# One block instead of three and a loop for a whole model, its weights fetched across the stages

## The reference, cut to what matters

```
for l in 0, 1:
    h = rmsnorm(x, norm_mix[l])
    u, q_lat, kv_lat, k_rope, hq, hf, hi, hg, gate_logits = split(h @ w_in[l])
    x += (g0 * s5(u) + g1 * mla(q_lat, kv_lat, k_rope) + g2 * hgrn2(hq, hf, hi, hg)) @ w_out[l]
    x += cross_attention(rmsnorm(x, norm_cross[l]), rmsnorm(mem, norm_mem[l]))   # keys: mem_n @ x_w_kv
    x += swiglu(rmsnorm(x, norm_ffn[l]), w_gate_up[l], w_down[l])
x = rmsnorm(x, norm_final)
for l in 0, 1:                                  # l = 0 the even part, l = 1 the odd part
    shift, scale, gate = split(silu(c) @ w_ada[l] + b_ada[l])     # "adaption"
    h = rms_norm(x, g[l]) * (1 + scale) + shift
    x += gate * (attention_l(h) @ w_out_l)      # even: sliding window and block-sparse; odd: block-sparse
out = rms_norm(x, final)
```

## Time and profile before

| what | before |
|---|---|
| median of 3 runs | 1708.95 us (1707.45 to 1709.88) |
| the profiled execution's own time | 1706.99 us |
| its span, first to last instruction | 1705.2 us |
| PE busy | 1633.9 us, 96% of the span |
| DVE, ACT, POOL busy | 837.5, 425.9, 9.1 us |
| mean granted clock of PE | 0.983 |
| moved by DMA | 244.16 MB, mean 143 GB/s |

### The profile page before, as it was taken

The page is one execution under the profiler, slowest core; times in us unless marked ns, Lnnn a source line. Parts: engine busy times, 40 slices in busy tenths (PEclk is TensorE's granted clock), DMA queues, the critical chain, the costliest instruction groups (busy, mean ns, idle before and its releaser), DMA issues. The chain is left out here.

```text
span 1705.2 us, 25659 instructions
## 1 busy us (share of the span) xinstructions
PE 1633.9 (96%) x10243; PEld 1378.0 (81%) x10243; DVE 837.5 (49%) x1646; ACT 425.9 (25%) x883; POOL 9.1 (1%) x24
## 2 busy tenths in 40 slices
PE   6999999999899998999999999899999899899997
PEld 5878868888899997868867888899998767676776
DVE  5346782324656754345792223667663454322332
ACT  5523423103111002423423203100001144411331
POOL 1000000000000001000000000000000000000000
PEclk9999999999999999999999999999999999899998
DMA  8442252353368553533352443467553525123310
GB/s 263 159 148 99 90 184 100 100 185 111 127 202 264 198 175 107 205 114 105 130 152 86 148 148 98 150 198 248 193 178 124 196 74 198 50 99 125 117 56 25
DMA packets 177659, 244.16 MB, mean 143 GB/s; under 512 B 22245, under 2 KB 100734, under 8 KB 177534
## 3 DMA queue, kind: packets, MB, share of 16 engines
q1 hardware_dynamic: 177534, 242.44, 42.6%
HBM read 241.37 MB, written 1.05 MB: 142 GB/s over the span
## 5 line engine op out<-in xcount | busy, mean ns | idle before, releaser
L566 PE MATMUL psum<-hT,ring 128*128 128x256 f32 (+1 forms) x2576 | 575.4, 383 | 9.1 <-DVE hT L2503 7.6
L566 PEld LDWEIGHTS psum<-hT,ring 128*128 128x128 f32 (+1 forms) x2576 | 488.0, 191 | 88.3 <-issue 20.1
L451 DVE TENSOR_TENSOR psum<-psum,const 128x512 f32<-128x512 f32 (+2 forms) x40 | 22.1, 570 | 162.7 <-PE psum L380 154.8
L1261 PE MATMUL psum<-hT,ring 128*128 128x128 f32 x704 | 86.4, 283 | 7.6 <-issue 7.6
L1261 PEld LDWEIGHTS psum<-hT,ring 128*128 128x128 f32 x704 | 84.4, 200 | 8.4 <-issue 8.4
L566 PE MATMUL psum<-uT,ring 128*128 128x256 f32 x384 | 85.6, 381 | 0.0
L566 PEld LDWEIGHTS psum<-uT,ring 128*128 128x128 f32 x384 | 72.5, 190 | 10.9 <-issue 0.7
L1446 ACT ACTIVATE SCR<-SCR 128x512 f32<-128x512 f32 x22 | 13.9, 630 | 223.8 <-DVEq L1886 223.8
L577 PE MATMUL psum<-ring,hT 128*128 128x512 f32 (+3 forms) x224 | 68.1, 459 | 0.0
L429 ACT ACTIVATE SCR<-psum,stats 128x128 f32<-128x128 f32 (+2 forms) x128 | 49.6, 398 | 44.9 <-DVE stats L465 39.0
L1643 DVE COPY_PREDICATED SCR<-levels,psum 128x512 f32<-128x512 uint8 x32 | 23.5, 734 | 73.8 <-PE psum L1025 73.1
(11 more groups left out here) (424 smaller groups left out, 2491.6 us busy)
## 6 DMA issues: line engine op xcount, KB each, us to landing
ring<-in_w_in SPq DMA_DIRECT2D x48, 1024.0 KB, 7.2
ring<-in_ffn_w_gate_up SPq DMA_DIRECT2D x88, 512.0 KB, 6.3
ring<-in_w_ada SPq DMA_DIRECT2D x24, 1024.0 KB, 5.9
ring<-in_ffn_w_down SPq DMA_DIRECT2D x16, 1024.0 KB, 8.0
ring<-in_w_in_odd SPq DMA_DIRECT2D x16, 1024.0 KB, 7.4
ring<-in_w_in_even SPq DMA_DIRECT2D x10, 1024.0 KB, 7.3
ring<-in_x_w_kv SPq DMA_DIRECT2D x8, 1024.0 KB, 5.2
ring<-in_ssm_w_glu SPq DMA_DIRECT2D x8, 1024.0 KB, 6.5
```

The costliest lines, as they stand in the source:

```text
L451: ins = nc.vector.tensor_tensor(pick(view), pick(view), mask[:, heads], ALU.add)
L566: ins = nc.tensor.matmul(b[0:width, n * S:n * S + S], w[k // 4][:, k % 4, c0[n]:c0[n] + width], src[:, k, :], start=k == 0, stop=k == kt - 1)
L1261: ins = nc.tensor.matmul(b[:, at:at + P], left, right, start=first, stop=last)
```

## The change

**One block.** `build` makes all job lists and the ring's list once, numbered on across the stages, and all stages stand in one `nc.Block`, with no barrier, loop or clearing of semaphores. Each stage has its own named semaphores. The parameters of layer 1 (`par[1]`) and of the second block are transposed in step 11 of the feed-forward before (job `next params`).

**Ring.** SP runs through one list of 232 pieces. The last pieces of layer 0 are followed by layer 1's kx, hf, hq, ql, whose slots come free with d12, d13 and d14; those of layer 1 by ada10, ada11, ada12 (two pieces each) and qa, of which ada12.1, qa.0 and qa.1 have slots that d14 frees. In the feed-forward the list is now `gate_up(0)`, six adaption pieces, `gate_up(1)`, and so on; so ff1.0 has the slot of ff0.0 and ff1.1 that of ff0.1.

**Start.** SP: half the constants, x, 15 small transfers, then the ring's hf.0 and hf.1, mem, other constants, raw b and c, then hq, kx, then levels, positions, the second block's parameters, ql and so on. PE: x0 to x3, params, square x, hf0, mem0 to mem3, square mem (from squares that ACT writes), hf1, hq0, hq1, kx0 left, kx0 right, kx1. DVE copies x out of PSUM and makes the rotary angles after its parameter chain; ACT copies and squares mem after its own parameter chain and hf0.

**Layer 1.** Order: kx0 left, square x, kx0 right, kx1, hf. Square x has 4 tiles: ACT squares x as the down steps finish it, DVE adds pairs. The memory's norm for layer 1 stands in down step 12.

**Adaption.** Three jobs a layer in the norm gap before the feed-forward (one before `square xf`'s sums, two behind), with their transposes in steps 0, 1, 2. Of the second block's six, three stand around its first squares, one in attention step 13, two behind `square 2`.

**Second block and end.** `square 0` and `square 1` have 4 tiles each. The output leaves in four DMAs of 256 KB, each behind its copy. As the jobs are numbered on across the stages, other jobs than before are the ones that need two successive banks at the turn of the six (mla1; c6, c7 before; mla3 in layer 0, a1 and b2's compression after).

The diff, cut to its core and with changes of indentation left out:

```diff
     def load(self, sp, before):
-            if n >= RING:
-                sp.wait_ge(self.jobs.done, self.jobs.at[self.pieces[n - RING][4]] + 1)
+            if n >= RING:
+                sp.wait_ge(self.done, self.pieces[n - RING][4] + 1)
...
+ADA_GAP = [[(0, 0), (0, 1), (0, 2)], [(0, 3), (0, 4), (0, 5)]]
...
-def layer_plan():
-    names = ["params", "square x", "kx0", "kx1"]
-    names += ["hf0", "hf1", "hq0", "hq1"]
+def layer_plan(layer, before):
+    if layer == 0:
+        names = [f"x{c}" for c in range(4)] + ["params", "square x", "hf0"] + [f"mem{c}" for c in range(4)]
+        names += ["square mem", "hf1", "hq0", "hq1", "kx0 left", "kx0 right", "kx1"]
+    else:
+        names = ["kx0 left", "square x", "kx0 right", "kx1", "hf0", "hf1", "hq0", "hq1"]
...
+    names += [f"ada{l}{n}" for l, n in ADA_GAP[layer]]
     for u in range(FF_STEPS + DOWN_STEPS):
-        names += [f"a{u}"] + ([f"ada{ada_at(u)}"] if ada_at(u) is not None else []) + [f"{x}{u}" for x in "bcd"]
+        names += [f"{x}{u}" for x in "abcd"] + (["next params"] if u == FF_STEPS else [])
...
-    for c in range(FF_STEPS):
...
-        ada(c)
+    gate_up(0)
+    for l, n in ADA_GAP[layer]:
+        wide(f"ada{l}{n}", a["w_ada_2"], 512 * n, 512, f"ada{l}{n}", l)
+    for c in range(1, FF_STEPS):
+        gate_up(c)
...
+    def sum_summed(name, source, squares, summed):
+        b = jobs.begin(pe, name)
+        pe.wait_ge(summed, 1)
+        for k in (0, 1):
+            nc.tensor.matmul(b[:, 0:S], ones, source(k), start=k == 0, stop=False)
+        pe.wait_ge(squares, 4)
+        for k in (6, 7):
+            ins = nc.tensor.matmul(b[:, 0:S], ones, source(k), start=False, stop=k == 7)
+        close(ins)
...
     sum_squares_after("square xf", sq, sig["squares"], 8, sig["summed"], layer + 2, [
...
-                for c in range(4)])
+            for c in range(4)], lambda: adaption(0))
+        adaption(1)
+        adaption(2)
...
+            forget(0)
+            for c in range(4):
+                copy(f"mem{c}", memT[:, 2 * c:2 * c + 2, :])
...
+            nc.scalar.activation(QKr[:, 0:2048], memT.rearrange("p k t -> p (k t)"),
+                                 ACT.Square).then_inc(sig["mem_squared"], 1)
+            root(rstd[:, S:2 * S], "square mem", slice(0, S), D).then_inc(sig["mem_root"], 1)
+            forget(1)
...
 def second_plan():
-    names = ["params", "square 0", "square 1", "qa0", "qa1", "ka", "va", "qa swap0", "qa swap1", "ka swap", "kw", "vw"]
+    names = ["ada10", "square 0", "square 1", "ada11", "ada12", "qa0", "qa1", "ka", "va", "qa swap0", "qa swap1", "ka swap"]
...
-        prologue(nc, a, m, sems)
-        restart()
-        with nc.Fori(0, DEPTH) as layer:
-            first_block_layer(nc, layer, a, m, sems)
-            restart()
-        second_block(nc, a, m, sems, out)
+        with nc.Block() as block:
+            load_weights(nc, block, a, m, sems, ring)
+            for layer in range(DEPTH):
+                first_block_layer(nc, block, layer, a, m, sems, books)
+            second_block(nc, block, a, m, sems, books, out)
...
+        put(m["const_tile"][:, 0:half_const], a["c_const"][:, 0:half_const], first["ident_in"])
+        input_in("x", m["QK"][:, 0:2048].rearrange("p (t n) -> p t n", t=TT))
+        load_rows(sp, 0, a, m, first["rows_in"])
+        ring.load(sp, {"0 hq.0": memory_in, "0 ql.0": tables_in, "0 glu gate.0": next_layer, "2 qb.0": small_params})
```

More of the change, by code:

```diff
@@ new lines, in _ @@
+        for n in range(2):
+            transposed(f"hq{n}", ["hq.0", "hq.1"], pair(n), hT, KT)
+        if layer == 0:
+            keys("kx0 left", (0,), (P,))
+            keys("kx0 right", (P,), (P,))
+            keys("kx1", pair(1))
+        for n, part in enumerate(("re", "im")):
+            b = jobs.begin(pe, f"bT {part}")
+            pe.wait_ge(sig["b_made"], n + 1)
+            for i in range(4):
+                ins = nc.tensor.transpose(b[:, i * P:(i + 1) * P], Bm[n][:, i * P:(i + 1) * P], ident)
+            close(ins)
@@ new lines, in gate @@
+        def gate(n):
+            transposed(f"gate{n}", [f"gate{n // 2}.0", f"gate{n // 2}.1"], pair(n), hT, KT)
+        for step in SSM_STEPS:
+            what, n = step.split() if " " in step else (step, "")
+            if step == "u1":
+                fill["u1"]()
+            elif step == "hg out":
+                hg_out()
+            elif step == "hg square":
+                hg_squares()
+            else:
+                {"bu": ssm_in, "gate": gate, "out": ssm_out}[what](int(n))
@@ new lines, in _ @@
+        half_vx("vx0 right")
+        for n in range(2):
+            transposed(f"xq{n}", ["xq.0", "xq.1"], pair(n), hT, KT,
+                       tile_ready=(sig["normed"], KT) if n == 0 else None)
+        jobs.evacuated(pe, "xq0")
+        jobs.evacuated(pe, "xq1")
+        for i in range(mem.steps):
+            if i == LAG + 1:
+                for name in ("vx0 left", "vx0 right", "vx1 left", "vx1 right"):
+                    jobs.evacuated(pe, name)
+            mem.pe(nc, pe, i)
+            for name in X_FILL.get(i, []):
+                half_vx(name)
@@ L2367, in _ @@
             warm()
             for c in range(4):
+                jobs.evacuated(act, f"{'even' if n == 2 else 'odd'} out{c}")
                 nc.scalar.activation(sq[:, 2 * c:2 * c + 2, :], xT[:, 2 * c:2 * c + 2, :],
                                      ACT.Square).then_inc(sig["squares"], 1)
[L2371 to L2378 removed]
@@ new lines, in _ @@
+        for name in ("q0", "k0", "v0", "v1"):
+            odd_copy(name)
+        for i in range(att_c.steps):
+            att_c.act(nc, act, i)
+            for name in C_FILL.get(i, []):
+                if name.startswith("silu"):
+                    silu(name[-1])
+                elif "swap" not in name and not name.startswith("part"):
+                    odd_copy(name)
+        square(3)
+        for n in range(4):
+            copy(f"final{n}", o_nat[:, n // 2, 512 * (n % 2):512 * (n % 2) + 512])
```

3079 lines of the change are left out of this document (1578 added, 1501 removed), and 2 rows, old and new, of the table AB_FILL.

## The result

The changed kernel takes 1684.22 us (median of 4 runs, 1682.91 to 1687.62); the kernel before, measured beside it, 1708.2 us (4 runs, 1706.01 to 1709.88). The ratio is 0.9865, with a 95% interval of 0.9854 to 0.9877: 24 us, or 1.35%, faster. The forecast was 1689 us, in a range of 1668 to 1700.

A forecast was written before the change was run, and what follows sets the result against it. TensorE was taken to bound the kernel, busy 1633.9 of 1705.2 us. The terms sum to -19.5 us, taking 1706.99 to 1687.5; with 1.96 for the median it said 1689 us, range 1668 to 1700.

The forecast's parts named there:

- start, to bT: Start until job bT: PE waits for ACT's parameter chain, copies and Square before square mem; bT at 74.9, +2.6 us.
- wait before the first level, two layers: Before the level jobs: ACT's angle functions now stand right ahead of them, 0.55 us a layer, +1.1 us.
- norm gap, two layers, with 3 jobs each: Gap before the feed-forward: three adaption jobs fill the idle time and leave the steps behind, a0 warm, -13.6 us.
- second feed-forward step, two layers: Before a1: PE waits for ff1's late pieces, then runs at a low clock; 9.5 us a layer, +19.0 us.
- first down step, two layers: First down step of the feed-forwards: no term in the sum; the transposes were said to only move.
- layer 0 to 1, and the parameter jobs: Barrier between the layers: 27.8 us shrink to 15.5 of keys and squares, less 0.3 for parameters, -12.0 us.
- layer 1 to the second block: Barrier before the second block: adaption jobs and squares fill the wait, qa0 no earlier than 10.7 us, -12.8 us.
- attention with ada13: Second block's attention: the adaption job is only moved, into a stretch that DVE paces, +0.8 us, bounds 0 and +2.
- even to odd: Passage from even to odd part: two adaption jobs fill idle time before q0 and leave the feed-forward, -2.8 us.
- output: End of the kernel: the last 256 KB lands sooner than the former 1 MB transfer, -1.8 us, bounds 0 and -1.8.
- ff1 stall: Wait before a1 because ff1's slots come free with c0 and d0: 7.5 us, plus 2.0 for the clock, each layer.
- rival of quicker transfers: Rival, 11%: ff1's last half lands in 3.9 us, so the wait before a1 is 4.8 us; 1682.6 us in all.

The follow-up runs named there:

- experiment 2: Changed kernel with ff1 fetched ahead of the adaption pieces, two adaption jobs left in the norm gap and the third before the first down step: 1667.2 us.
- experiment 3: Changed kernel with 17 more matmuls before a1 in both layers, where PE waited for ff1: 1682.86 us.
- Experiment 4: Changed kernel, still without barriers, with layer 1's and the second block's first pieces fetched only after the stage before has done its last job: 1709.04 us.
- experiment 6: No kernel of its own: one even attention stretch compared over eight profiles, the changed kernel and others alike there; it took 166.5 to 170.9 us.

## Why the prediction was right

The sum was -19.5 us against the profiled span, and the profile shows -24.1. The terms, read from the two profiles by the same starts and ends:

| term | predicted | measured |
|---|---|---|
| start, to bT | +2.6 | +3.1 |
| wait before the first level, two layers | +1.1 | +0.9 |
| norm gap, two layers, with 3 jobs each | -13.6 | -12.6 |
| second feed-forward step, two layers | +19.0 | +18.2 |
| first down step, two layers | 0 | +3.2 |
| layer 0 to 1, and the parameter jobs | -12.0 | -11.5 |
| layer 1 to the second block | -12.8 | -12.3 |
| attention with ada13 | +0.8 | -6.6 |
| even to odd | -2.8 | -3.1 |
| output | -1.8 | -2.0 |
| sum | -19.5 | -22.7 |

The total came as near as it did partly by luck: the attention is 7.4 us off its term one way and the first down step 3.2 the other way. 1.4 us of the 24.1 stay without a place; some 0.8 of it is that an adaption job took 1.86 us of a feed-forward step and I had booked 1.79.

**The ff1 stall** was right in place, cause and size. The prediction took its size from one row, and the runs show what lies behind that row: ff1's slots come free only with c0 and d0, and its 2.1 MB then take some 6 us at 344 GB/s. Idle times of 6.82 and 7.01 us stand where 7.5 was forecast, and a1's loss is 2.26 and 2.08 where I took 2.0; experiment 2 shows the cause, experiment 3 that the second number is the clock. By the Trainium skill's fit ("DMA: Bandwidth & Descriptors", section "Anatomy of one DMA", which gives it for transfers that GpSimd issues; SP issues these) this term had been estimated at +14. Here the fit was too short: the last half landed 6.2 and 6.4 us after its issue, not 3.2, and the sum taken from the rows was nearer. The rival of quicker transfers, 4.8 us, is out: with this order of slots and nothing put into the wait, it was 6.8 us or more in every profile.

**The borders** came within 0.5 us each, by the steps given: 64 key instructions and four tiles of squares in the first, and the third piece behind d14 in the second. Experiment 4 shows what the prediction had only argued, that nearly nothing of it comes without the fetching.

**The start** was right in its mechanism. The gap was sized at 6 us where it was 7.69, since PE came to it sooner; what counts is that it ended at 34.33, 0.7 us before the 35.0 of the forecast, because x had landed 1.5 us sooner than I took from mem's row. Square mem took 6.67 us instead of 5.4, and half of that loss came back so.

**The attention term failed.** It was +0.8 and came out as -6.6, which is more than the whole miss of 5 us. The step in the prediction was "The job itself is only moved", with +0.8 for a stretch that DVE paces. But a stretch that DVE and ACT pace is one where PE waits, and there a job of PE's is hidden: the waits of 0.73, 0.71 and 0.59 of the 0.90 us went away (2.0 us). The other 4.5 us are the same instructions at the full clock, by the rows 5.82 against 3.72, 1.52 against 0.85 and their like, and experiment 6 shows that this part is luck and not the change's: of the seven other profiles with the same instructions there, six have the low clock at the first place and all seven at the second. With the middle of the eight stretches, 169.2 us, the term would be about -4 (an estimate), still not +0.8. The medians are 24.0 us apart as well, from executions of 1682.9 to 1687.6 us; how much of that is the same chance, one profile of the kernel before can't say.

**The first down step** wasn't in the sum. With the adaption of step 10 gone, PE reaches it sooner against DVE and waits 2.10 us instead of 1.66, and then ran 22 instructions in 3.84 and 4.03 us, not 2.72. The prediction said "The transposes (0.44 each) only move", booked the jobs' own time, and never asked what the six removed jobs had covered where they stood. Only 0.9 of the 3.2 us is the wait. The rest is the clock: in the seven other profiles with the same wait these 22 instructions took 2.72 us in layer 1 six times and 4.35 once, and in layer 0 2.72 twice and 3.81 to 4.35 five times. Experiment 2 fills the wait.

## What to carry to other kernels

When a piece is put earlier into the order of a ring, look at which pieces fall behind it, and at the job that frees each one's slot: a fetch is late if that job stands right ahead of its reader, here 18 us for an advantage of 12.6, and another order of the pieces, with one job moved, made the two stretches 21.7 us shorter. The value of joining these stages was in what is fetched across their borders; with the barriers gone and no fetching ahead, 1.2 us were won at one border and 3.2 lost at the other. And a filler job is worth the wait that it covers: count waits also in the places where it is put down and where it is taken away.

## What the runs showed of the hardware

The granted clock after a short wait isn't the same in every profile. After waits of 1.45 us between the same instructions, 16 matmul instructions ran in 3.72 us in two of the profiles and in 5.41 us or more in the others, and stretches of some 169 us spread by 4.4 us, mostly for this and for the clock behind a second wait. A difference of 2 to 4 us between single profiles of this kernel says nothing until the clock of the stretch is read beside it. And the transfer of the same half megabyte in the same place landed from 6.2 to 8.2 us after its issue over the profiles; holding back what stood behind it gave 6.6 twice. While PE waited for it, the DMA share was 1.05 at 344 GB/s, and the longer waits had more bytes of the later pieces in them, 0.4 to 0.9 MB.
